# Modulation units of a hybrid backbone kernel, moved from the FFN output projections into the input projections

## The reference, cut to what matters

```python
def modulation(cvec, w, b):
    m = jax.nn.silu(cvec) @ w + b
    return m.reshape(cvec.shape[0], N_SUB, 3, 1, D_MODEL).transpose(1, 2, 0, 3, 4)

def ffn_sublayer(x, mod_j, g_pre, g_post, w_in, w_out):
    h = pre(x, mod_j, g_pre)
    return x + MACARON_W * mod_j[2] * rmsnorm(swiglu(h, w_in, w_out), g_post)
```

## Time and profile before

| | |
|---|---|
| median of three runs | 3012.33 us |
| span of the profiled execution | 3013.7 us |
| mean granted clock of TensorE over the span | 0.961 |
| TensorE busy | 2740.7 us, 91% |
| VectorE, ScalarE, GpSimd busy | 23%, 17%, 6% |
| chain that ended last, share on TensorE | 83% |
| HBM read | 255.87 MB, 85 GB/s over the span |

### The profile page before, as it was taken

The page is one execution under the profiler, slowest core; times in us unless marked ns, Lnnn a source line. Parts: engine busy times, 40 slices in busy tenths (PEclk is TensorE's granted clock), DMA queues, the critical chain, the costliest instruction groups (busy, mean ns, idle before and its releaser), DMA issues.

```text
span 3013.7 us, 27300 instructions
## 1 busy us (share of the span) xinstructions
PE 2740.7 (91%) x10207; PEld 1513.3 (50%) x10207; DVE 681.4 (23%) x1393; ACT 520.2 (17%) x816; POOL 190.8 (6%) x260
## 2 busy tenths in 40 slices
PE   4999999899968888888899999899999979968998
PEld 1444433244457767783344433334443435736887
DVE  1100000255146555661300000120000030162001
ACT  1000000222142233212100000110000020173111
POOL 1000011000011121110000001100001000010000
PEclk7999999999979999999999999999999989998999
DMA  6222466222200000002122256422226303102452
GB/s 228 80 74 78 117 200 191 91 81 72 68 4 1 0 0 0 1 1 77 56 83 70 86 164 197 138 70 70 84 80 182 106 30 98 56 0 98 152 167 72
DMA packets 243277, 257.75 MB, mean 86 GB/s; under 512 B 6297, under 2 KB 223891, under 8 KB 243091
## 3 DMA queue, kind: packets, MB, share of 16 engines
q1 hardware_dynamic: 222483, 181.43, 19.6%
q0 software_dynamic: 20736, 75.51, 7.9%
HBM read 255.87 MB, written 1.05 MB: 85 GB/s over the span
## 4 chain that ended last, share of the span: by engine, by line
PE 83%; DVE 6%; issue 5%; ACT 4%; DMA 1%; DVEq 1%; POOL 0%; SPq 0%; ACTq 0%; POOLq 0%
PE bank L576 35%; PE bank L537 31%; PE bank L511 3%; PE bank L728 2%; PE bank L726 2%; PE bank L809 2%; PE bank L711 2%; DVE hs L1335 1%; PE bank L660 1%; ACT L888 1%; DMA mring<-in_w_mod 1%; DVE hs L1483 1%; PE bank L747 1%; PE bank L831 1%; DVE hs L1156 1%
## 5 line engine op out<-in xcount | busy, mean ns | idle before, releaser
L576 PE MATMUL bank<-hs,ring 128*128 128x512 f32 (+1 forms) x2816 | 1069.8, 542 | 23.6 <-DVE hs L1161 23.6
L576 PEld LDWEIGHTS bank<-hs,ring 128*128 128x128 f32 x2816 | 536.9, 191 | 553.5 <-issue 520.5
L537 PE MATMUL bank<-big,ring 128*128 128x512 f32 (+1 forms) x1664 | 651.9, 542 | 9.1 <-POOL big L449 5.5
L537 PEld LDWEIGHTS bank<-big,ring 128*128 128x128 f32 x1664 | 307.6, 191 | 296.0 <-issue 272.5
L537 PE MATMUL bank<-hs,ring 128*128 128x512 f32 (+2 forms) x784 | 319.0, 570 | 12.9 <-DVE hs L1161 12.7
L1173 DVE TENSOR_TENSOR big<-bank,room 128x512 f32 (+1 forms) x88 | 55.0, 625 | 993.8 <-PE bank L576 993.8
L537 PEld LDWEIGHTS bank<-hs,ring 128*128 128x128 f32 (+1 forms) x784 | 151.3, 194 | 180.5 <-issue 169.2
L917 ACT ACT_TABLE_LOAD x44 | 56.5, 1283 | 747.3 <-PE bank L576 747.3
L402 POOL DMA_DIRECT2D mring<-in_w_mod x144 | 76.2, 529 | 1473.2 <-PE bank L511 1470.4
L1091 ACT ACTIVATE hs<-bank 128x512 f32 (+1 forms) x48 | 25.2, 526 | 724.4 <-PE bank L537 724.4
L711 PE MATMUL bank<-mring,hs 128*128 128x128 f32 x768 | 106.0, 284 | 19.4 <-DVE hs L1335 19.4
(11 more groups left out here) (202 smaller groups left out, 1774.6 us busy)
## 6 DMA issues: line engine op xcount, KB each, us to landing
ring<-in_ffn_w_in SPq DMA_DIRECT2D x88, 1024.0 KB, 5.0
mring<-in_w_mod POOLq DMA_DIRECT2D x144, 512.0 KB, 4.0
ring<-in_ffn_w_out SPq DMA_DIRECT2D x32, 1408.0 KB, 7.1
ring<-in_gdn_w_in SPq DMA_DIRECT2D x16, 1024.0 KB, 5.6
ring<-in_diff_w_in SPq DMA_DIRECT2D x12, 1024.0 KB, 5.1
ring<-in_gdn_w_out SPq DMA_DIRECT2D x4, 1024.0 KB, 5.2
ring<-in_diff_w_out SPq DMA_DIRECT2D x4, 1024.0 KB, 5.2
cst<-in_consts SPq DMA_DIRECT2D x1, 1600.0 KB, 7.1
```

The source lines that it names most:

```text
L537: last = mm(bank[0:rows, r % 4, 0:cols], w[:, k, :], rhs(k), start=(k == 0), stop=(k == n_k - 1))
L576: last = mm(bank[:, (g0 + 2 * v + jj) % 4, 0:TOK - c0], w[:, k, jj * P:(jj + 1) * P], hs[:, k, c0:TOK], start=(k == 0), stop=(k == KC - 1))
```

## The change: bursts of four units between groups

The output projections lose all their modulation units. The input projections of the same three FFNs carry them, in bursts of four units with no matmul of the projection between them. In the first and the last two pairs (`whole_vector`) a pair takes a whole vector: a burst behind its first group, one behind its third, the turn behind its fourth. In the loop over pairs 1 to 8 two pairs share a vector: a burst behind the fourth group of the first, a burst behind the second group of the second, the turn behind its fourth. FFN 0 takes vectors 2 to 8, FFN 2 vectors 9 to 14, FFN 3 vectors 15 to 17, as before. Each burst has the units 0 to 3 or 4 to 7 of a vector, so it uses each slot of `mring` once. `mod_unit`, `mod_turn` and the loads of GpSimd and SyncE are not changed.

```diff
-MOD_GATE = 8
-MOD_INSIDE = {0: 48, 2: 48, 3: 24}
+MOD_PAIRS = {0: {0: 2, "loop": 3, 9: 7, 10: 8}, 2: {"loop": 9, 9: 13, 10: 14}, 3: {0: 15, 9: 16, 10: 17}}
...
-                    def pair(i, a, fresh=False, with_mod=False):
+                    vecs = MOD_PAIRS.get(n, {})
+
+                    def mod_four(i, half):
+                        for k in range(4):
+                            mod_unit(i, 4 * half + k)
+
+                    def whole_vector(i):
+
+                        return ((0, lambda: mod_four(i, 0)), (2, lambda: mod_four(i, 1)), (3, lambda: mod_turn(i)))
+
+                    def pair(i, a, fresh=False, after=()):
...
-                                    if with_mod and k % 4 == 2:
-                                        mod_unit(MOD_FIRST // KC, 4 * v + 2 * jj + k // 4)
                                 last.then_inc(S["acc_done"], 1)
+                                for q, what in after:
+                                    if q == 2 * v + jj:
+                                        what()
...
-                    with pe.Fori(0, FC // 4) as it:
-                        pair(it * 2, 0, fresh=True)
-                        pair(it * 2 + 1, 2)
-
-                    pair(FC // 2 - 1, FC // 4 * 4, with_mod=(n == 0))
-                    if n == 0:
-                        mod_turn(MOD_FIRST // KC)
+                    pair(0, 0, fresh=True, after=whole_vector(vecs[0]) if 0 in vecs else ())
+                    with pe.Fori(0, FC // 4 - 1) as it:
+                        if "loop" in vecs:
+                            i = it * 1 + vecs["loop"]
+                            pair(it * 2 + 1, 2, after=((3, lambda: mod_four(i, 0)),))
+                            pair(it * 2 + 2, 4, after=((1, lambda: mod_four(i, 1)), (3, lambda: mod_turn(i))))
+                        else:
+                            pair(it * 2 + 1, 2)
+                            pair(it * 2 + 2, 4)
+                    for i in (9, 10):
+                        pair(i, 2 * i, after=whole_vector(vecs[i]) if i in vecs else ())
...
-                    def out_four(it, with_mod):
-
+                    with pe.Fori(0, 2) as it:
                         for r in range(4):
-                            def between(k, r=r):
-
-                                hidden_wait(k)
-                                if with_mod and k % 3 == 2 and k < 18:
-                                    m = 6 * r + k // 3
-                                    mod_unit(it * 3 + (mod0[n] // KC + m // KC), m % KC)
                             unit_wait(uo + it * 4 + r, uo + r)
                             group(go + it * 4 + r, go + r, slot(uo + r, FC, P), lambda k: big[:, k, 0:TOK - c0],
-                                  cols=TOK - c0, starts=True, ready=between)
-                            if with_mod and r > 0:
-                                mod_turn(it * 3 + (mod0[n] // KC + r - 1))
...
+                    def single(i):
+                        if i in vecs:
+                            mod_rows(vecs[i])
+                        products(i)
+                        if i in vecs:
+                            mod_columns(vecs[i], vecs[i] // 9)
+
+                    single(0)
+                    with dve.Fori(0, FC // 4 - 1) as it:
+                        products(it * 2 + 1)
+                        if "loop" in vecs:
+                            mod_rows(it * 1 + vecs["loop"])
+                        products(it * 2 + 2)
+                        if "loop" in vecs:
+                            mod_columns(it * 1 + vecs["loop"], 0 if vecs["loop"] < 9 else 1)
+                    single(9)
+                    single(10)
...
-                        if with_mod and r > 0:
-                            vec = it * 3 + (mod0[n] // KC + r - 1)
-                            mod_rows(vec)
-                            mod_columns(vec, 0 if mod0[n] // KC < 9 else 1)
                         dve.wait_ge(S["out_squared"], n * KC + it * 4 + r + 1)
```

More of the change, by code:

```diff
@@ L149, in hybrid_backbone @@
     places, n_const = constant_places()
-    unit0, group0, mod0 = [], [], {}
+    unit0, group0 = [], []
     u = g = 0
-    m = MOD_FIRST + MOD_GATE
     for n, (kind, _, _) in enumerate(SUBS):
@@ L158, in hybrid_backbone @@
         g += GROUPS[kind]
[L159 to L162, removed]
     ffns = [n for n, s in enumerate(SUBS) if s[0] == "ffn"]
@@ L599, in hidden_wait @@
                             pe.wait_ge(S["acc_freed"], go + 2 * (k - (FC - 2)) + 2)
-                    def out_four(it, with_mod):
+                    with pe.Fori(0, 2) as it:
                         for r in range(4):
-                            def between(k, r=r):
-                                hidden_wait(k)
-                                if with_mod and k % 3 == 2 and k < 18:
-                                    m = 6 * r + k // 3
-                                    mod_unit(it * 3 + (mod0[n] // KC + m // KC), m % KC)
                             unit_wait(uo + it * 4 + r, uo + r)
                             group(go + it * 4 + r, go + r, slot(uo + r, FC, P), lambda k: big[:, k, 0:TOK - c0],
-                                  cols=TOK - c0, starts=True, ready=between)
-                            if with_mod and r > 0:
-                                mod_turn(it * 3 + (mod0[n] // KC + r - 1))
[L616 to L622, removed]
+                                  cols=TOK - c0, starts=True, ready=hidden_wait)
                 if kind == "gdn":
@@ L1167, in _, with products @@
                     s0 = ffns.index(n) * FC
-                    with dve.Fori(0, FC // 2) as i:
+                    vecs = MOD_PAIRS.get(n, {})
+                    def products(i):
                         for jj in range(2):
@@ L1174, in _ @@
                                              sg[:, jj, 0:width].unsqueeze(1), ALU.mult).then_inc(S["acc_freed"], 2)
-                    if n == 0:
-                        mod_rows(MOD_FIRST // KC)
-                        mod_columns(MOD_FIRST // KC, 0)
+                    def single(i):
[14 more added lines that the diff above has]
+                    single(10)
                     go = g0 + 2 * FC
@@ L1452, in _ @@
                 steps.link(v_.memset(ssq[:, :], 0.0))
-                def out_four(it, with_mod):
+                with dve.Fori(0, 2) as it:
                     for r in range(4):
-                        if with_mod and r > 0:
-                            vec = it * 3 + (mod0[n] // KC + r - 1)
-                            mod_rows(vec)
-                            mod_columns(vec, 0 if mod0[n] // KC < 9 else 1)
                         dve.wait_ge(S["out_squared"], n * KC + it * 4 + r + 1)
@@ L1464, in out_four @@
                                          ).then_inc(S["acc_freed"], 1)
[L1466 to L1472, removed]
                 dve.wait_ge(S["m_ready"], m + 3)
```

## The result

The changed kernel takes 3157.36 us (median of 4 runs, 3154.14 to 3163.58) against 3012.7 us of the kernel before in the same session: ratio 1.0486, 95% interval 1.0471 to 1.0501. The forecast was 3176 us. The profiled execution took 3154.14 us and has a span of 3152.2 us, 138.5 more than before.

The account below looks back on a forecast made before the run. TensorE's queue was taken to bound the kernel (busy 91%). 32 x (6.31 + 1.8) = 259.5, less 94.7 and 1.3, gives +163.5 us on the 3013.7 us span, so 3177; forecast 3176 us, range 3116 to 3222.

Parts of the forecast that it names:

- Removed units: Output projections and the first FFN's last input-projection pair: 128 scattered units at 0.74 us each, 94.7 us go.
- The missing credit: In 32 input-projection bursts the fourth unit's load waits for the first unit's start; 6.31 us per burst at full clock.
- The landing: Load of each burst's fourth unit: 4.3 us from issue to data, with 3.7 and 5.2 as ends.
- The clock: TensorE behind each burst: the stop lowers its clock, 1.8 us lost each time, 57.6 us over 32 bursts.
- (a): The stops at the bursts are there but TensorE's clock mostly holds: +105.9 us, 3118 us; chance 0.12.
- (b): Modulation and weight loads collide at the bursts, landings go to 6.3 us: +64 us, 3240 us; chance 0.09.
- (c): All four loads are there when a burst begins: 2.03 us per burst, 2981 us; chance 0.02.
- (d): Bursts split up on TensorE's queue, so the change doesn't do what it says; dismissed, no size or chance of its own.
- At nothing: VectorE's copies and adds between input-projection products, and the loads' order, cost nothing; 11 us if the copies' cover were gone.

Follow-up runs that it names:

- the scattered kernel: The changed kernel's placement in the input projections, but one unit at a time, three credits: 3011.98 us, ratio 0.9996 to the kernel before.
- the two early kernels: The changed kernel with each burst's first unit two matmuls, or one matmul, ahead of the other three: 3048.41 us and 3114.2 us.

## Why the prediction was right, point by point

**Removed units.** 0.74 us each: the scattered kernel has the same spacing at another place and the same time within 0.1%. The sum assumed that the place costs nothing, and that is shown.

**The missing credit.** Predicted from the earlier trace rows as a wait in each of 32 bursts. All 32 have it, and with a fourth credit all are gone. Idle time ahead of the modulation line was to grow by about 131 us; by group 5 of the page it grew by 127.0 - 17.7 = 109.

**The landing.** This is the term that was mis-sized: 4.3 us taken, 4.9 - 1.24 - 0.03 = 3.63 measured, below the 3.7 that I had as the lower end from the earlier trace rows. 32 x 0.67 = 21 us too much. In spans the forecast stood 25 us too high (3177 against 3152.2): 21 by the landing, 2 by the clock (taken as the rest of the balance below) and 2 by a start that happened to be shorter. The median of the runs stands 5 us above the profiled span, where the forecast had it 1.4 below, so the forecast of 3176 looks closer than it was, 19 us off. The step that failed is the one that put the value between the 4.0 of the earlier trace rows and the 4.5 of the earlier trace rows, although it said that the weight queue would be empty at every burst. The load of the earlier trace rows was not alone, as the trace of the kernel before shows for SyncE's queue between its issue and its landing (27.19 to 31.74 us; packets, MB, share):

```profile
q1 hardware_dynamic: 458, 0.46, 28.4%
```

Moving the bursts behind a weight load brings 4.5 us back, and 6.4 beside output weights, the 6.3 of the earlier trace rows. The Trainium skill, page "DMA: Bandwidth & Descriptors", section "Anatomy of one DMA — SWDGE (gpsimd) path", by whose fit 512 KB take an estimated 3.2 us, lay closer to these loads than my value did, though under the 3.4 of the shortest one.

**The clock.** 1.8 us per burst taken; the windows give 1.9, and the span's balance (below) 1.74. It holds as a mean over falls of two sizes (1.5 to 1.7 and 2.7 to 3.1 us), which the prediction did not foresee; that its mean came so near is in part luck, since it was taken from four pauses of 2.98 to 5.50 us. Which stop is needed was left open and is narrowed by the two early kernels. The Trainium skill, page "TensorE: Matmul & The Clock Gate", section "HAM oscillation — how this bites in real kernels", tells of just this pattern, one DMA wait and one fall of the clock per trip of a loop, and the trace agrees with it: 30 of 32 bursts.

**The balance** of the profiled span: 32 x (0.20 + 4.9 + 0.54) = 180.5, less 94.7 and 1.3, is 84.5; the start was 1.8 us shorter (72.39 against 74.18); 138.5 - 84.5 + 1.8 = 55.8 remain, which I put down to the clock, 1.74 us per burst; the windows, which are independent of this sum, give 59.

**Rivals.** (a), the clock holds, is refuted at this stop and true at 1.6 us. (b), loads that collide, did not occur; where the burst stands behind a weight load it does, in the full size of 6.3 us in nine bursts only: 3210 us. (c), all loads there at the start of a burst, came true in the kernel that supplies what it was said to need, a fourth credit: 2976 us where 2981 were worked out (some 3 us of that come from the start, as the kernel before with four credits shows). (d) is refuted by the timeline.

**At nothing.** VectorE's copies between the products delayed no group: with the stops gone (four credits) TensorE had no idle time in 370 us of this stage, the first FFN.

## What to carry to other kernels

A ring of slots whose hand-back is tied to the start of the next use has one credit less than slots. That costs nothing while the uses are spread out and costs a whole landing as soon as as many uses as slots stand together; so bunch up to the number of credits, or hand back at the end of the use. Bunching by itself pays here (0.51 us per unit in four, 0.54 in three, 0.74 alone), and four credits with bursts of four beat both kernels by 1.2% and more. Keep what is left of a stop short: at 1.6 us it cost its length, at 2.2 two thirds more, at 3.4 half as much again.

## What the runs showed of the hardware that was not expected

In the changed kernel the fall of the clock behind a burst has two sizes, 1.5 to 1.7 us lost or 2.7 to 3.1, and none between; with the burst behind a weight load, where the stops are longer, there are some between (0.64 to 0.74 over 7 us). A stop of 2.08 us brought it down where one of 2.26 in the same kernel did not, so these runs have no single length of stop at which it falls. In the burst at 170.49 us the fourth unit still ran at full clock (0.61 us) while the mean of the 7 us from its start is 0.76: the fall can come after the stop has ended. A stop is therefore not judged by the instruction right behind it.

The changed kernel's runs go from 3154.14 to 3163.58 us, with mean granted clocks of 0.943, 0.942, 0.940 and 0.940 in the order of their times, so at least part of this scatter goes with the clock. It does not take such stops: the runs of the kernel with bursts of three, which has none, go from 2985.6 us at a clock of 0.960 to 2996.31 at 0.953. Where those runs lost it is not shown, since only one execution of each kernel has a trace.
